# Two stage boundaries rewritten: norms by quarters, a fourth unit in the opening block, and quad operands prepared ahead of the norm

## The chip, the cores and the metric

The kernel runs on one core of one Trainium2 chip. The metric is device time in microseconds (us) for one execution. TensorE is called PE, VectorE DVE, ScalarE ACT, GpSimd POOL, and SyncE, which only issues transfers here, SP.

## The reference

One inference step of one layer over 640 tokens (512 of a prompt, 8 streams of 16), width 1024, all in fp32:

```
x <- LN1(alpha*x + 0.5*SwiGLU_1(x))
p = x @ W_in          # conv B, C, H | q | k | v | g | gate_conv | gate_ret
y_c = (B * causal_conv3(C*H)) @ W_conv_br
y_r = (groupnorm(retention(q, k, v)) * silu(g)) @ W_ret_br      # 4 heads, rotary q and k
h = (sigmoid(gate_conv)*y_c + sigmoid(gate_ret)*y_r) @ W_out
x <- LN2(alpha*x + h)
x <- LN3(alpha*x + 0.5*SwiGLU_2(x))
```

It also returns the last convolution inputs and the retention states.

## The kernel before

**Products.** Every fp32 operand is split in a high part (`xh`, `wh`: rounded copy, made by ACT or by a converting DMA) and a low part (`xl`, `wl`: the rest, made by DVE or POOL). A product is three matmuls, low*high, high*low, high*high (`mm3`, line 776; the matmul itself is line 771). The chip has one pass of some 110 numbered weight chunks of 128x1024: SP loads the raw chunk, POOL issues the DMA of its high part (`high`, L675), then makes its low part (`low`, L684). A chunk sits in one of three ring slots, or in an extra slot (3, 4: `raw_x`, `wh_x`, `wl_x`) that lies over the tiles `th`, `tl` when these are dead; `EXTRA_SLOT` says which chunks do, `slot_free` what a load waits for, `release_order` in which order the chunks come free.

**Stages.** FFN 1; the projections; four retention heads; the output product; FFN 2. The up products of both FFNs and the projections are mostly made as *quads* (a seven-product scheme over two halves of the tokens and of the rows). A quad needs four sums `n1, n2, t3, t4` of quarters of x (`x_sums`, tiles `t32`, `th`, `tl`), and six weight operands A11, S12, A12, S3, A22, S4: quarters of a loaded block `qraw`, and sums of them in `qs` (`quad_s`). POOL makes two of these sums (`sums`, L697 and L701), DVE two (`second_sum`, `fourth_sum`), ACT the high parts (`quad_hi_part`), DVE the low parts (`quad_lo_part`). The first products of a stage are plain *units* of one chunk (128 output rows, two halves of 320 tokens, 24 matmuls each).

**A boundary** (between FFN 1 and the projections, here boundary A, and between the output product and FFN 2, boundary B) ends one stage with a layer norm and starts the next:

- PE ends with the products `last_down` (A) or `out_products` (B). They serve tokens in two sets, *early* (tiles 0 to 2) and *late* (3 and 4), so that DVE can normalise the early ones while PE works on the late ones.
- DVE (`end_stage`): adds the residual (`down`, L1968), `bn_stats` (L2002), the inverse deviation, then two instructions a tile for scale and shift (L2014, L2017), which signal `z_ready`.
- PE transposes z tile by tile in two pieces of four 128x128 blocks (`to_T`, L1084; 6 early pieces, later 4 late ones). ACT copies each piece to `xh`, DVE makes `xl` from the piece and `xh` (signal `x_low`), ACT then copies the piece whole to `xin` (signal `x_kept`), which `x_sums` reads. A PSUM bank is free after that.
- PE runs `IDLE_UNITS` = 8 matmuls on a tile of ones after the early pieces, then the first three units (`first_units`) over the first half of the tokens; at `LATE_AT` (before the last k of unit 3) it transposes the late pieces; then it runs the second half of the three units, then a fourth unit in both halves, then quads (A) or the first down products (B, `first_down`, which wait for `h_ready`).
- POOL makes the low parts of the first chunks only after `z_ready` of the early tiles, that of the fourth after all tiles.
- The six operands of a stage's first quad are made after the norm; at B between the first units and the down products.

Each engine has its own instruction list and runs it in order. Nothing reorders work; counts of semaphores (`wait_ge`) join them.

Of the kernel before, what the change touches and what calls it, by code (L numbers as in the profile page):

```python
# [48 lines left out]
FIRST_IN_DEAD = (SECOND - DOWN_PARTS + 2, LAST - OUT_PARTS + 1, LAST - OUT_PARTS + 2)  # L49
# [194 lines left out]
EARLY_PIECES = [(t, q) for t in range(EARLY) for q in range(2)]  # L244
# [3 lines left out]
def transposed_bank(b, t, q):  # L248

    return b if t < EARLY else (b + 5 + LATE_PIECES.index((t, q))) % 8  # L250
# [13 lines left out]
def build_layer(nc, a):  # L264
# [3 lines left out]
    with ctx:  # L268
# [130 lines left out]
        for n, (raw_at, hi_at) in enumerate(((t_at[3], t_at[1]), (t_at[0], t_at[2]))):  # L399
# [21 lines left out]
        pool_sums, dve_sums = sem("pool_sums"), sem("dve_sums")  # L421
# [25 lines left out]
        x_kept, x_low = sem("x_kept"), sem("x_low")  # L447
# [86 lines left out]
        def _(sync):  # L534
# [26 lines left out]
            def ffn(k):  # L561
# [8 lines left out]
                if k == 1:  # L570
                    sync.wait_ge(merged_ready, KT)
                    for slot in range(4):
                        sync.wait_ge(state_out[slot], 32 * H)
                load_quad(2 * k)
                load_quad(2 * k)
                load(3)
                for g in range(1, len(GROUPS)):
                    into_dead = (k, g) == (0, len(GROUPS) - 1)
                    load(2)
                    load_quad(2 * k)  # L580
                    if not into_dead:
                        load(1)
                    for _ in range(3):
                        load_quad(2 * k)
                    load(2 if into_dead else 1)
# [69 lines left out]
            load(KT)  # L655
            ffn(1)
# [9 lines left out]
        def _(pool):  # L666
# [37 lines left out]

            def ffn(k):
                if k == 1:
# [5 lines left out]
                sums(2 * k)  # L712
                if k == 1:
# [8 lines left out]
                for g in range(1, len(GROUPS)):  # L722
                    into_dead = (k, g) == (0, len(GROUPS) - 1)
                    high(ck(2 if into_dead else 3))
                    for part in range(3):
# [3 lines left out]
                        if into_dead and part == 2:  # L729
                            high(ck(2))  # L730
                        low()
                    sums(2 * k)
                    low()

            def projections():
                sums(1)
# [6 lines left out]
                low()  # L743
                sums(1)
# [11 lines left out]
            low()  # L756
            ffn(1)
# [1728 lines left out]
```

## Time and profile before

| | |
|---|---|
| median of 3 runs | 1802.85 us (1801.83 to 1803.66) |
| profiled execution, its own time | 1801.98 us |
| its span in the trace | 1799.8 us |
| PE busy | 1777.6 us, 99% |
| DVE, ACT, POOL busy | 71%, 36%, 30% |
| DMA share at boundary B, before the output product ends | 16 engines all busy, 407 GB/s |

Slices of the profile show PE at 90% or more from start to end, so the time is PE's own work plus the places where it waits or runs products that serve nothing. Idle time of any other engine costs nothing by itself.

### The profile page before, as it was taken

The numbers are of one execution on the slowest core, as the hardware profiler recorded it, in microseconds if no ns is written. First come the engines' busy times: TensorE is split into PE (matmuls) and PEld (weight loads), VectorE is DVE, ScalarE is ACT, GpSimd is POOL, SyncE is SP. The second block draws the span as 40 slices with busy tenths as digits, with TensorE's granted clock in tenths as the row PEclk, the third lists the DMA queues.
The fourth block names the chain that finished last, engine by engine and source line by source line (L and its number), as shares of the span: only waits on it lengthen the run. The fifth ranks groups of instructions, "written<-read, shape, count | busy, mean of one in ns | idle before, by whom it ended". The sixth has DMA issues, their size and how long they took to land.

```text
span 1799.8 us, 26971 instructions
## 1 busy us (share of the span) xinstructions
PE 1777.6 (99%) x10868; PEld 1656.8 (92%) x10868; DVE 1281.2 (71%) x1698; ACT 645.0 (36%) x1102; POOL 541.1 (30%) x360
## 2 busy tenths in 40 slices
PE   9999999999999999999999999999999999999997
PEld 8989899898999999999998979798989989899896
DVE  7958485667798787776257666767867868485675
ACT  5425233242545454544106050514205325242242
POOL 2324242224232222121341323232244324233231
PEclk9999999999999999999999999999999999999998
DMA  7342423325443333422764958586964332323313
GB/s 272 129 141 71 141 73 132 123 71 199 146 143 127 115 130 101 143 87 91 273 240 140 339 200 312 204 284 231 345 258 158 129 135 77 129 82 129 114 63 106
DMA packets 89419, 287.33 MB, mean 160 GB/s; under 512 B 8784, under 2 KB 11216, under 8 KB 89040
## 3 DMA queue, kind: packets, MB, share of 16 engines
q1 hardware_dynamic: 48176, 171.72, 28.3%
q0 software_dynamic: 15552, 56.63, 9.2%
q10 hardware_dynamic: 25568, 57.26, 8.7%
q8 instruction: 87, 1.43, 0.3%
q14 instruction: 36, 0.29, 0.0%
HBM read 244.35 MB, written 42.28 MB: 159 GB/s over the span
## 4 chain that ended last, share of the span: by engine, by line
PE 91%; DMA 3%; POOL 1%; issue 1%; DVE 1%; ACT 1%; DVEq 0%; POOLq 0%
PE ps L771 90%; DMA wh<-in_weights 2%; PE ps L1141 1%; POOL wl L684 1%; DMA wh_x<-in_weights 1%; ACT xh L1282 0%; POOL wl_x L684 0%; DVE y L2075 0%; DVE z L2064 0%; PE ps L1084 0%; DVE y L2084 0%; ACT xin L1282 0%; DVE rt L1682 0%; DVE xl L1682 0%; DVE mv L2070 0%
## 5 line engine op out<-in xcount | busy, mean ns | idle before, releaser
L771 PE MATMUL ps<-th,wql 128*128 128x320 f32 x1136 | 350.9, 309 | 0.0
L771 PE MATMUL ps<-th,wqh 128*128 128x320 f32 x1136 | 350.7, 309 | 0.0
L771 PE MATMUL ps<-tl,wqh 128*128 128x320 f32 x1136 | 350.0, 308 | 0.0
L684 POOL TENSOR_TENSOR wl<-raw,wh 128x1024 fp32r<-128x1024 f32 x101 | 257.3, 2549 | 97.7 <-DMA wh<-in_weights 70.6
L1282 ACT ACTIVATE pu<-ps 128x320 f32<-128x320 f32 x213 | 93.3, 438 | 522.7 <-PE ps L771 522.6
L1682 DVE TENSOR_TENSOR wql<-qraw,wqh 128x512 fp32r<-128x512 f32 x213 | 259.9, 1220 | 17.3 <-ACT wqh L1282 17.1
L771 PE MATMUL ps<-xl,wqh 128*128 128x320 f32 x852 | 262.7, 308 | 0.0
L771 PE MATMUL ps<-xh,wqh 128*128 128x320 f32 x852 | 262.6, 308 | 0.0
L771 PE MATMUL ps<-xh,wql 128*128 128x320 f32 x852 | 262.5, 308 | 0.0
L697 POOL TENSOR_TENSOR quad_s<-qraw 128x512 f32<-128x512 f32 x71 | 93.7, 1319 | 485.2 <-DVE wql L1682 449.0
L1682 DVE TENSOR_TENSOR wql<-quad_s,wqh 128x512 fp32r<-128x512 f32 (+1 forms) x213 | 194.3, 912 | 45.3 <-ACT wqh L1282 44.5
L771 PEld LDWEIGHTS ps<-tl,wqh 128*128 128x128 f32 x1136 | 213.3, 188 | 0.4
L771 PEld LDWEIGHTS ps<-th,wql 128*128 128x128 f32 x1136 | 213.2, 188 | 0.4
L771 PEld LDWEIGHTS ps<-th,wqh 128*128 128x128 f32 x1136 | 213.2, 188 | 0.0
L675 POOL DMA_DIRECT2D wh<-in_weights x101 | 56.8, 563 | 515.2 <-PE ps L771 415.4
L1282 ACT ACTIVATE wqh<-quad_s 128x512 fp32r<-128x512 f32 (+1 forms) x213 | 163.8, 769 | 50.2 <-PE ps L771 50.2
L771 PE MATMUL ps<-wh,hl 128*128 128x512 f32 x430 | 168.2, 391 | 0.5 <-DVE sig L1682 0.2
L771 PE MATMUL ps<-wh,hh 128*128 128x512 f32 x430 | 167.6, 390 | 0.0
L771 PE MATMUL ps<-wl,hh 128*128 128x512 f32 x430 | 167.6, 390 | 0.0
L771 PEld LDWEIGHTS ps<-xl,wqh 128*128 128x128 f32 x852 | 160.0, 188 | 0.4
L771 PEld LDWEIGHTS ps<-xh,wql 128*128 128x128 f32 x852 | 159.9, 188 | 0.4
L771 PEld LDWEIGHTS ps<-xh,wqh 128*128 128x128 f32 x852 | 160.0, 188 | 0.0
(221 smaller groups left out, 3440.8 us busy)
## 6 DMA issues: line engine op xcount, KB each, us to landing
qraw<-in_quads SPq DMA_DIRECT2D x142, 512.0 KB, 3.6
raw<-in_weights SPq DMA_DIRECT2D x105, 512.0 KB, 3.8
wh<-in_weights POOLq DMA_DIRECT2D x101, 512.0 KB, 5.5
state<-in_state_ret ACTq DMA_DIRECT2D x32, 512.0 KB, 6.7
out_ret_sample<-state ACTq DMA_DIRECT2D x32, 512.0 KB, 5.2
state<-in_state_ret SPq DMA_DIRECT2D x16, 512.0 KB, 5.3
qk_scratch<-ctp SPq DMA_DIRECT2D x8, 640.0 KB, 5.4
swish_scratch<-ctp SPq DMA_DIRECT2D x6, 640.0 KB, 3.0
```

The source lines that it names most:

```text
L675: pool.dma_start(w_hi(r), a["weights"][c]).then_inc(hi_loaded[r], 16)
L684: pool.tensor_tensor(w_lo(r), w_raw(r), w_hi(r).bitcast(f32), ALU.subtract).then_inc(chunk_split, 1)
L697: pool.tensor_tensor(qs[:, 0, :], qraw[:, c0, 512:1024], qraw[:, c1, 512:1024], ALU.add).then_inc(pool_sums, 1)
L771: ins = nc.tensor.matmul(out, lhs, rhs, start=start, stop=stop, skip_group_check=adds)
L1141: last = nc.tensor.transpose(cols(k, 128, ps[:, b, :]), src, ident[:, :])
L1282: return nc.scalar.activation(out, in_, ACT.Copy, **kw)
L1682: return V.tensor_tensor(out, x, y, op)
```

## The change

It touches the two boundaries only; the arithmetic is the same.

- Four units instead of three (`FIRST_UNITS`) stand in the opening block, first halves first. The 8 idle products are gone.
- Unit 0 begins with the high*high products of quarter 0 (k 0 to 3), which need four high copies and one bank; then high*low, then quarter 1, and its chunk's low part last. Copies and low parts are ordered by quarters to match (`HIGH_ORDER`, `LOW_ORDER`, `natural_part`), and the transposed pieces lie in other banks (`EARLY_BANK`). Hence PE waits, ahead of the first transposition, until DVE has freed all but two banks.
- The fourth unit's products with the high part of its chunk stand before the late transpositions, the ones with its low part behind them.
- `second_sum` and `fourth_sum` of the first quad of the projections and of FFN 2 move from DVE to POOL (`all_sums`). At A it stands before the last `low` of FFN 1, at B behind the last `low` of the output product.
- Their six operands: ACT's high parts move ahead of the norm. DVE's low parts move too: at A two ahead of the norm, one behind the late shift, one behind the late `xl` pieces, two where they were; at B all six between the first and the second half of the early residual sums.
- The four loads of the first two quads of FFN 2 move on SP from behind three raw chunks of FFN 2 to right behind the last raw chunk of the output product; the loads of `z_kept` 3 and 4 move on ACT behind the first PSUM results of the output product.
- The last chunk of FFN 1 (25) instead of the third last (24) takes the extra slot; it is loaded after P7 of the last quad and not after P4. The extra slots' places over `tl` and the release order change with it. `x_sums` makes only n1 before the first chunk's release.

```diff
-FIRST_UNITS = 3
+FIRST_UNITS = 4
-IDLE_START, IDLE_UNITS = 24, 8
-LATE_AT = (FIRST_UNITS - 1, 7)
-DOWN_LATE, OUT_LATE = (2, 0, 1, 3), (1, 0, 3, 4, 2)
-EXTRA_SLOT = {SECOND - DOWN_PARTS + 2: NSPL, SECOND: NSPL,
+DOWN_LATE, OUT_LATE = (3, 0, 2, 1), (1, 0, 3, 4, 2)
+EXTRA_SLOT = {SECOND - 1: NSPL, SECOND: NSPL,
...
+T_HIGH_ORDER = (0, 2, 1, 3)
+T_LOW_ORDER = [(0, 1, 2, 3) if stage == 1 else (0, 2, 1, 3) for stage in range(3)]
+EARLY_PIECES = [(0, 0), (1, 0), (0, 1), (1, 1), (2, 0), (2, 1)]
+HIGH_ORDER = [(0, 0), (1, 0), (0, 1), (2, 0), (1, 1), (2, 1)]
+LOW_ORDER = [(t, q) for q in range(2) for t in range(EARLY)]
+EARLY_BANK = {(0, 0): 2, (1, 0): 4, (2, 0): 0, (0, 1): 1, (1, 1): 3, (2, 1): 5}
+HIGHS_BEFORE = {q: 1 + max(n for n, piece in enumerate(HIGH_ORDER) if piece[1] <= q) for q in range(2)}
...
-                engine.wait_ge(chain_full, chained(QUADS - 1, P4))
+                engine.wait_ge(chain_full, chained(QUADS - 1, P7))
...
             load(KT)
+            sync.wait_ge(merged_ready, KT)
+            for slot in range(4):
+                sync.wait_ge(state_out[slot], 32 * H)
+            load_quad(2)
+            load_quad(2)
             ffn(1)
...
+            def all_sums(stage):
+                n = qk.at
+                sums(stage)
+                pool.wait_ge(pool_sums, 2 * n + 1)
+                pool.tensor_tensor(qs[:, 1, :], qs[:, 0, :], quad_source(n, A11), ALU.add).then_inc(later_sums, 1)
+                pool.wait_ge(later_sums, 2 * n + 1)
+                pool.wait_ge(quad_ready, operand(n - 1, S4))
+                pool.tensor_tensor(qs[:, 3, :], qs[:, 1, :], quad_source(n, A12), ALU.add).then_inc(later_sums, 1)
...
                 high(ck(2))
                 low()
             low()
+            all_sums(2)
             ffn(1)
...
             def to_T(pieces):
-                kept = zr.at // TT * 2 * TT
+                if pieces is EARLY_PIECES:
+                    pe.wait_ge(psum_free, bk(EARLY - TT))
...
-                if pieces is EARLY_PIECES:
-                    pe.wait_ge(x_low, kept + 1)
-                    pe.wait_ge(x_kept, kept + 1)
-                    idle_products(IDLE_UNITS, bk(-2 * EARLY) % 8)
...
+                pe.wait_ge(hi_loaded[s0], 16 * loads_of_slot(ck.at, FIRST_HI))
+                pe.wait_ge(x_kept, kept + 1)
+                for q in range(2):
+                    ks = range(4 * q, 4 * q + 4)
+                    pe.wait_ge(x_high, kept + HIGHS_BEFORE[q])
+                    for k in ks:
+                        products(0, 0, k, (0, 0), k == 0, False)
+                    pe.wait_ge(x_low, kept + EARLY * (q + 1))
+                    for k in ks:
+                        products(0, 0, k, (0, 1), False, False)
+                assert chunk() == s0
+                for k in range(KT):
+                    products(0, 0, k, (1, 0), False, k == KT - 1)
...
+                for k in range(KT):
+                    products(u, 0, k, (0, 0), k == 0, False)
+                    products(u, 0, k, (0, 1), False, False)
+                late_tiles()
+                assert chunk() == s
+                for k in range(KT):
+                    products(u, 0, k, (1, 0), False, k == KT - 1)
+                for u in range(FIRST_UNITS):
+                    pe.wait_ge(x_kept, kept + 2 * EARLY + u + 1)
...
             act.wait_ge(sp_out, 16 * H)
+            act.wait_ge(psum_full, bk(EARLY))
+            for t in range(EARLY, TT):
+                kept_load(t)
+            for what in (A11, S12, A12, S3, A22, S4):
+                quad_hi_part(QUAD_START[2], what)
             bk.add(2 * TT)
             roots_and_to_T()
...
+                if k == 1:
+                    quad_lo_part(PROJ, A11)
+                    quad_lo_part(PROJ, S12)
                 for t in early:
                     if residual is z_kept:
                         dve.wait_ge(z_kept_in[t], 16)
                     down(scale, 0, [t], residual)
                     moments(0, [t])
+                if k == 2:
+                    for what in (A11, S12, A12, S3, A22, S4):
+                        quad_lo_part(QUAD_START[2], what)
                 for t in early:
                     down(scale, 1, [t], residual)
                     moments(1, [t])
...
                 inv_deviation(late)
                 scale_and_shift(late)
+                if k == 1:
+                    quad_lo_part(PROJ, A12)
                 to_T(LATE_PIECES)
+                if k == 1:
+                    quad_lo_part(PROJ, S3)
                 transposed_freed(k, late)
```

## Rows read from the trace of the kernel before

**Rows 1.** Timeline of PE at boundary A: start, us, engine, line, operation; idle before

```profile
416.75 0.50 PE L771 MATMUL ps<-wh_x,hl 128*128 128x512 f32 x1 [0.87 <-POOL wl_x L684]
...
435.93 2.78 PE L1084 MATMUL ps<-ident,z 128*128 128x128 f32 x24
440.24 1.41 PE L771 MATMUL ps<-ones 128*128 128x320 f32 x8 [1.53 <-ACT xin L1282]
441.49 0.31 PE L771 MATMUL ps<-xh,wl_x 128*128 128x320 f32 x1
...
455.02 0.41 PE L771 MATMUL ps<-xh,wl_x 128*128 128x320 f32 x1 [0.84 <-ACT xin L1282]
...
472.72 0.31 PE L771 MATMUL ps<-xh,wql 128*128 128x320 f32 x1
```

**Rows 2.** Timeline of ACT at boundary A

```profile
436.56 3.05 ACT L1282 ACTIVATE xh<-ps 128x512 fp32r<-128x512 f32 x6 [9.07 <-PE ps L1084]
439.44 3.11 ACT L1282 ACTIVATE xin<-ps 128x512 f32<-128x512 f32 x6
...
452.24 2.24 ACT L1282 ACTIVATE xh<-ps 128x512 fp32r<-128x512 f32 x4 [6.29 <-PE ps L1084]
```

**Rows 3.** Timeline of DVE at boundary A

```profile
418.44 0.69 DVE L1968 SCALAR_TENSOR_TENSOR z<-ps,z 128x512 f32<-128x512 f32 x1 [3.98 <-PE ps L771]
...
437.42 3.67 DVE L1682 TENSOR_TENSOR xl<-ps,xh 128x512 fp32r<-128x512 f32 x6
```

**Rows 4.** Timeline of POOL at boundary A

```profile
452.17 2.38 POOL L684 TENSOR_TENSOR wl<-raw,wh 128x1024 fp32r<-128x1024 f32 x1 [7.49 <-DVE z L2017]
```

**Rows 5.** Timeline of PE at boundary B

```profile
1353.95 2.78 PE L1084 MATMUL ps<-ident,z 128*128 128x128 f32 x24
...
1372.88 0.42 PE L771 MATMUL ps<-xh,wl_x 128*128 128x320 f32 x1 [0.90 <-DVE xl L1682]
...
1390.58 0.39 PE L771 MATMUL ps<-wh,hl 128*128 128x512 f32 x1
```

**Rows 6.** Timeline of POOL at boundary B

```profile
1331.92 2.40 POOL L684 TENSOR_TENSOR wl<-raw,wh 128x1024 fp32r<-128x1024 f32 x1 [0.19 <-DMA wh<-in_weights]
...
1359.97 1.29 POOL L697 TENSOR_TENSOR quad_s<-qraw 128x512 f32<-128x512 f32 x1
...
1384.16 0.53 POOL L675 DMA_DIRECT2D wh<-in_weights  x1 [2.95 <-PE ps L771]
1385.70 2.42 POOL L684 TENSOR_TENSOR wl<-raw,wh 128x1024 fp32r<-128x1024 f32 x1 [1.02 <-DMA wh<-in_weights]
```

**Rows 7.** Timeline of ACT at boundary B, operand S12 of FFN 2's first quad

```profile
1384.12 1.05 ACT L1282 ACTIVATE wqh<-quad_s 128x1024 fp32r<-128x1024 f32 x1
```

**Rows 8.** Timeline of DVE at boundary B and behind it

```profile
1337.82 0.69 DVE L1968 SCALAR_TENSOR_TENSOR z<-ps,z_kept 128x512 f32<-128x512 f32 x1 [12.84 <-PE ps L771]
...
1351.57 1.28 DVE L2017 SCALAR_TENSOR_TENSOR z<-z,rt,lnb 128x1024 f32<-128x1024 f32 x1
...
1386.47 2.34 DVE L1682 TENSOR_TENSOR hl<-h,hh 128x640 fp32r<-128x640 f32 x1 [0.81 <-ACT hh L1282]
...
1392.79 0.82 DVE L1682 TENSOR_TENSOR hl<-h,hh 128x640 fp32r<-128x640 f32 x1 [0.81 <-ACT hh L1282]
...
1399.66 1.22 DVE L1682 TENSOR_TENSOR wql<-quad_s,wqh 128x1024 fp32r<-128x1024 f32 x1
```

**Rows 9.** Busy time by stretch: PE, PEld, DVE, ACT, POOL, clock, DMA, GB/s

```profile
1322.00:1328.00 6.00, 5.57 (x26) 4.29 (x24) 2.92 (x5) 0.00 (x0) 2.61 (x3) 1.00 1.06 407
...
1788.00:1790.00 2.00, 0.26 (x2) 0.00 (x0) 1.93 (x7) 0.48 (x3) 0.61 (x1) 1.00 0.94 96
1790.00:1792.00 2.00, 0.00 (x0) 0.00 (x0) 2.00 (x2) 1.16 (x2) 0.00 (x0) 0.66 1.07 201
```

**Rows 10.** Timeline of SP at the end of the output product

```profile
1312.84 7.13 SPq L542 DMA_DIRECT2D raw<-in_weights  x2
```

**Rows 11.** Timeline of PE at the start of the kernel

```profile
1.26 5.67 PE L771 MATMUL ps<-ones 128*128 128x320 f32 x24 [1.26 <-DVE ones L2130]
```

More of the change, by code:

```diff
@@ L569, in ffn @@
                 load(2)
[L570 to L575, printed above, removed]
+                if k == 0:
+                    load_quad(0)
+                    load_quad(0)
                 load(3)
                 for g in range(1, len(GROUPS)):
-                    into_dead = (k, g) == (0, len(GROUPS) - 1)
                     load(2)
                     load_quad(2 * k)
-                    if not into_dead:
-                        load(1)
+                    load(1)
                     for _ in range(3):
                         load_quad(2 * k)
-                    load(2 if into_dead else 1)
+                    load(1)
             def spill(q):
@@ L728, in ffn @@
                             pool.wait_ge(c22_made, QUAD_START[2 * k] + QUADS - 1)
-                        if into_dead and part == 2:
-                            high(ck(2))
                         low()
-                    sums(2 * k)
+                    if (k, g) == (0, len(GROUPS) - 1):
+                        all_sums(1)
+                    else:
+                        sums(2 * k)
                     low()
             def projections():
-                sums(1)
                 high(ck(4))
@@ L1054, in ffn @@
                     idle_products(IDLE_START, 0)
-                for u in range(0 if first else FIRST_UNITS, 4):
-                    unit_of_chunk(x_wait=x_piece if first and u == 0 else None)
+                for u in range(FIRST_UNITS if first else 0):
+                    unit_of_chunk(x_wait=x_piece if u == 0 else None)
                 n = 0 if first else QUAD_START[2]
@@ L1103, in first_units, with products @@
                 own, kept = bk.at, (zr.at - EARLY) * 2
-                slots = []
-                w_ofs = [lambda k, u=u: (cols(k, 128, w_hi(slots[u])), cols(k, 128, w_lo(slots[u])))
-                         for u in range(FIRST_UNITS)]
-                def before_half(half):
-                    pass
+                used = []
+                def products(u, half, k, which, start, stop):
+                    s, c = used[u], slice(half * HALF, (half + 1) * HALF)
+                    w_part, x_part = which
+                    w_of, x_of = (w_hi(s), w_lo(s))[w_part], (xh, xl)[x_part]
+                    return mm(ps[:, (own + 2 * u + half) % 8, 0:HALF], cols(k, 128, w_of), x_of[:, k, c], start, stop)
                 def late_tiles():
@@ L1126, in before_unit @@
+                for u in range(1, FIRST_UNITS - 1):
+                    used.append(chunk())
+                    if u == 1:
+                        pe.wait_ge(x_kept, kept + 2)
                     else:
                         pe.wait_ge(psum_free, own - 10)
[L1129 to L1134 removed]
@@ L1331, in window @@
                 bk.add(2)
-                quad_hi_part(n, A11)
-                quad_hi_part(n, S12)
+                if ffn == 0:
+                    quad_hi_part(n, A11)
+                    quad_hi_part(n, S12)
                 plain_hi(2 * ffn)
-                for what in (A12, S3, A22, S4):
-                    quad_hi_part(n, what)
+                if ffn == 0:
+                    for what in (A12, S3, A22, S4):
+                        quad_hi_part(n, what)
                 act.wait_ge(psum_free, bk())
@@ L1902, in projections @@
                 banks_freed(4)
-                for what in (A11, S12, A12, S3, A22, S4):
-                    quad_lo_part(n, what)
+                quad_lo_part(n, A22)
+                quad_lo_part(n, S4)
                 second_sum(n + 1)
@@ L2028, in end_stage @@
                     moments(0, [t])
+                if k == 2:
+                    for what in (A11, S12, A12, S3, A22, S4):
+                        quad_lo_part(QUAD_START[2], what)
                 for t in early:
@@ L2123, in to_T, with highs @@
                        xh[:, part[0], part[1]].bitcast(f32), ALU.subtract).then_inc(x_low, 1)
+                bk.add(len(pieces))
+            def highs(low, piece):
+                return low if piece in LATE_PIECES else (low - 1) // (2 * TT) * 2 * TT + HIGH_ORDER.index(piece) + 1
             def first_low_part(c, made, part=slice(0, D)):
```

173 lines of the change are left out of this document (98 added, 75 removed).

## The prediction

> **What bounds the kernel now.** I read the page first: PE is busy 99% of the span, so only what PE waits for, or runs for nothing, can be won. The timeline of PE then shows where that is. At boundary A [rows 1] PE waits 0.87 us for chunk 24's low part (DVE's sums follow PE there: DVE had been idle 3.98 us when it began, rows 3). It then transposes 24 blocks (2.78 us), waits 1.53 us, runs 8 products of ones that serve nothing, and starts real products at 441.49, 5.56 us after the first transposition. Behind the late transpositions it waits once more, until 455.02. Boundary B [rows 5] has the same shape: transpositions from 1353.95, the second halves only at 1372.88, the first down product at 1390.58. In sum some 5 us at A and 4.5 us at B can be won, 0.5% of the time. The rest of the trace matters only where the change makes another engine late. For that I read the timelines of ACT, DVE, POOL and SP around both boundaries [rows 2 to 4, 6 to 8, 10]. A product of 320 columns costs 0.147 us: from 455.02 to 472.72 there are 120 of them [rows 1].
>
> **Boundary A.** Times here count from the first transposition, T = 435.93 in the trace.
>
> *Chunk 24.* It no longer lies in the extra slot, so its data are there long before. Chunk 25 does, but its load starts one product group earlier (P7, not P4: 12 products of 0.147 and six of the lead, some 3 us) and PE needs it 4 us later than chunk 24. POOL's sums for the first quad of the projections stand in a stretch in which POOL waits. Won: 1.0 us (the start-to-start gap is 1.25 us where 0.23 is usual). DVE's two early low parts, 0.6 and 1.2 us, fit in its 3.98 us of idle time [rows 3]; without that cover they would cost 1.8 us.
>
> *Start of unit 0.* ACT's first copy starts at +0.63 and each takes 0.51 [rows 2], the pieces arrive every 0.44. The fourth high copy is that of the fifth piece: 2.4 to 3.0. The natural copy of the first piece follows, 2.9 to 3.5, and PE starts at +3.7 instead of +5.56. DVE's low parts go from +1.49 at 0.61 each [rows 3]: the third is done at 3.7, in time; the sixth waits for ACT's last high copy (4.5) and is done at 5.6, where PE is at 5.4. Unit 0 ends at 7.4 instead of 9.1.
>
> *Units 1 to 3.* Two units of 3.53, then 16 products: +16.8 (it was +15.8). The late tiles are shifted at +16.2, where POOL starts the fourth low part [rows 4], so the 16 transpositions run without a wait and end at +18.6. But DVE's low part of A12 now stands right there, too, and reads two SBUF operands as POOL does. Rows 8 show what that means: `hl` next to POOL's `low` [rows 6] took 2.34 us, alone 0.82. I let POOL lose the 0.7 us: its part is ready at 19.35, 8 products end at 20.6. The first natural copy of a late piece lets PE go 2.78 after ACT's first late copy [rows 1, 2], here at +20.2, earlier. So the second halves start at 20.6 with 96 products left: 34.7. Before: 455.02 is +19.1, with 120 left: +36.8. Won: 2.1 us. The next in line is DVE: it must wait for chunk 26's release (24.1), make three x sums and four low parts (4.2 and 5.7 us) before it frees the units' banks, at about +34.3; 0.4 us of slack are left, which I cost at nothing.
>
> A gives 3.1 us, between 1.5 (POOL and bank late by 0.8 each) and 4.
>
> **Boundary B.** This is where I expect the change to pay back. `all_sums` stands behind the last `low` of the output product, which ends at 1334.3 [rows 6]. All six low parts of the first quad's operands stand on DVE between the early tiles' first and second halves, and DVE starts the second half at 1337.82, having waited 12.84 us for PE [rows 8]. The chain that must now fit between the two: POOL's sums at 1.28 each [rows 6], the third of which S12 needs (3.9 us), ACT's high part of S12 (1.05, rows 7), DVE's low part of it (1.22, rows 8), and four more at 0.61 with the gaps of signals: 8.7 us in all. From 1334.3 that ends at 1343.0. And POOL's last `low` will be later: until 1328 the 16 DMA engines are fully busy at 407 GB/s [rows 9], and behind the last raw chunk (about 1319.6 to 1320, rows 10) SP now issues four loads of 512 KB, 5.2 us of all engines; the last high part's DMA shares with them. I put it at 1.1 us (nothing to 2.2). So DVE begins its second half at 1344.1, 6.3 us late.
>
> What follows, by the distances of the old trace: the residual of the late tiles' first half is done at 1350.2 + 6.3 = 1356.5 (L2017 of tile 2, rows 8, ends at 1352.85, and the shift's two instructions take 2.6 of it). PE waits for it now ahead of its transpositions, for which it is ready at 1353.95 or some 0.5 earlier: 3 us of idle time. Tile 2 is shifted at 1359.1, two `bn_stats` follow (1.3), the first `xl` 0.65, the natural copy 0.6: unit 0 starts at 1361.9. From there PE needs 96 products, 1.85 us of transpositions and two short waits (0.5 at the sixth `xl`, 0.5 at the late natural copy): the second halves start at 1378.8, and end at 1392.9, where before they ended at 1390.58.
>
> Then the down products start, and all before them has less cover than it had: three units of second halves were followed by 48 products, now by one unit. The high parts of the down chunks need the slots of units 1 and 2: before, the second was issued at 1384.16 and the low part made from 1385.70 [rows 6], 11.3 and 12.8 us after the second halves' start; that is 1391.6 to 1394.0 now. On DVE and ACT `x_sums` wait for unit 0 (1382.6), then three sums, the last high part, a table load, sigmoid and the plain tile give `h_ready` at 1394.0, plus 0.75 for `hl` next to POOL's `low`, as in rows 8. The second down chunk's low part costs 0.4 more. The down products so start at 1394.8, effectively 1395.3: B loses 4.7 us, between 2.5 (no DMA delay, no collision) and 6.
>
> The Trainium skill states this collision as a rule (page "SBUF — State Buffer", section "SBUF: two separate sides"): GpSimd and a DVE instruction with two SBUF inputs take one port in turn, whole instructions long. The trace agrees, 2.34 against 0.82 us. By a kernel without it, the sum would be 1.1 us less.
>
> **The sum** is made against the profiled execution: 1801.98 - 3.1 + 4.7 = 1803.6. That execution was 0.87 below the median of the runs, so I forecast 1804.4, 0.1% above the median. A measurement of this kernel can tell some 0.2%, 3.6 us, from no change. The bounds give 1801.5 to 1806.9 as the likeliest case's own range.
>
> **The rivals.**
>
> *The norm at B is not delayed.* POOL would have to finish its sums before 1333 or so, or DVE the operands in its idle time. The same sums move at A, and there they fit. Against it: at B the sums stand behind a `low` that ends at 1334.3 in the trace. Then B is as A: unit 0 starts 1.9 us sooner and the idle products are gone, 2.4 us, and 0.6 for the wait of a chunk in the output product. Sum: -3.1 - 3.0 = 1796.7. Chance 0.12.
>
> *The clock falls at B.* At the end of the trace PE's last product ends at 1788.26, and the granted clock is 1.00 until 1790 and 0.66 on average to 1792 [rows 9]: it went from 2.4 to 1.2 GHz some 2.4 us behind the last product. The gaps of 1.53 us it held through. By my sum PE is idle for 3 us ahead of the transpositions and twice more up to unit 0. At half rate the first 24 products of the kernel took 5.67 us instead of 3.53 [rows 11], 2.1 us more; the tail of the transpositions adds up to 0.9. That gives 1804.4 + 3.0 = 1807.4, slower. It decides from the point where PE's gap exceeds about 2.4 us. Against it: transpositions run in between, and the fall may end before unit 0 starts, and then costs under 1 us. Chance 0.22. The Trainium skill, page "TensorE: Matmul & The Clock Gate", section "Why this matters for your kernels", warns of just this: idle gaps between bursts of products bring the half clock back. No row before has a gap as long within the kernel.
>
> *A gives only chunk 24's 1.0 us.* POOL and DVE collide longer, or the banks come late. Then 1806.5. Chance 0.1.
>
> The forecast itself: 0.56.
>
> **Numbers.** Faster by over 0.2% (below 1799.2) is the first rival and little else: 0.13. Slower (above 1806.5): two thirds of the clock's case, half of the third rival, a tenth of the forecast: 0.27. The same: 0.60. The range leaves out the first rival and the clock's worst: 1800 to 1808.
>
> **What the profile will show.** Right: no wait for `wl_x` near 415; PE's first `xh` product 3.7 us behind the first transposition at A and the first quad 34.7; at B DVE's first residual with `z_kept` of the second half near 1344 behind `wql` low parts, an idle PE of some 3 us ahead of the transpositions, and a wait of the first down product for POOL's or DVE's part. Wrong: DVE's second half at B still started by PE at about 1337; or `quad_s` on POOL done before 1335; or PE waiting at A for a bank ahead of the first quad, or for chunk 25.

## The result and the profile after

| | before | changed |
|---|---|---|
| median, both timed in turn on one chip, 20 runs each | 1803.34 us (1801.38 to 1805.25) | 1806.20 us (1804.67 to 1808.69) |
| ratio, with its 95% interval | | 1.0018 (1.0011 to 1.0024) |
| profiled execution, its span | 1801.98, 1799.8 us | 1808.0, 1806.2 us |

The change costs 0.18%, inside what I called "the same" (0.2%), and lies in the forecast range. The changed kernel's profiled execution is 1.8 us above its own median, the one before 1.4 below its own, so the traces show a larger difference, 6.0 us, than the medians, 2.9. Small numbers from one trace are therefore checked against a second trace of the same kernel (`t_again` below).

**Boundary A** went as planned but for one wait. The timeline of PE in the changed kernel, to be read beside [rows 1]:

```profile
416.02 0.47 PE L796 MATMUL ps<-wh,hl 128*128 128x512 f32 x1 [0.39 <-DVE hl L1754]
...
435.19 2.78 PE L1116 MATMUL ps<-ident,z 128*128 128x128 f32 x24
438.75 0.83 PE L796 MATMUL ps<-xh,wh_x 128*128 128x320 f32 x4 [0.78 <-ACT xin L1338]
...
454.25 1.43 PE L796 MATMUL ps<-xh,wl 128*128 128x320 f32 x8 [0.29 <-POOL wl L698]
...
469.71 0.39 PE L796 MATMUL ps<-xh,wql 128*128 128x320 f32 x1
```

Counted from the first transposition, unit 0 starts at +3.56 (5.56 before), the last 8 products ahead of the second halves at +19.06, the first quad at +34.52. The first quad comes at 469.71 and not at 472.72: 3.0 us. But chunk 24 still waits, now for `hl`, and the reason stands in the timelines of DVE and of POOL:

```profile
409.76 3.16 DVE L1754 TENSOR_TENSOR ct<-ct,ct 128x1280 f32<-128x1280 f32 x1
```
```profile
409.17 2.39 POOL L698 TENSOR_TENSOR wl_x<-raw_x,wh_x 128x1024 fp32r<-128x1024 f32 x1 [4.38 <-DMA wh_x<-in_weights]
```

DVE's product of two SBUF tiles took 3.16 us; the same one took 1.49 in the kernel before, where POOL made no low part at that time:

```profile
410.01 1.49 DVE L1682 TENSOR_TENSOR ct<-ct,ct 128x1280 f32<-128x1280 f32 x1
```

The early low part of chunk 25 made it late, and `hl` behind it.

**Boundary B** went as feared, and further. The timelines of PE [rows 5], POOL [rows 6], ACT [rows 7] and DVE [rows 8], now:

```profile
1325.56 0.50 PE L796 MATMUL ps<-wh_x,xl 128*128 128x512 f32 x1 [1.43 <-POOL wl_x L698]
...
1355.85 1.97 PE L1116 MATMUL ps<-ident,z 128*128 128x128 f32 x16 [2.80 <-DVE z L2041]
1358.58 1.06 PE L1116 MATMUL ps<-ident,z 128*128 128x128 f32 x8 [0.77 <-DVE z L2090]
1360.95 1.35 PE L796 MATMUL ps<-xh,wh_x 128*128 128x320 f32 x4 [1.31 <-ACT xin L1338]
...
1394.68 0.50 PE L796 MATMUL ps<-wh,hl 128*128 128x512 f32 x1 [1.62 <-DVE hl L1754]
```
```profile
1325.46 0.58 POOL L689 DMA_DIRECT2D wh<-in_weights  x1
...
1332.62 2.39 POOL L698 TENSOR_TENSOR wl<-raw,wh 128x1024 fp32r<-128x1024 f32 x1 [2.19 <-DMA wh<-in_weights]
1334.97 1.29 POOL L711 TENSOR_TENSOR quad_s<-qraw 128x512 f32<-128x512 f32 x1
1336.22 1.30 POOL L715 TENSOR_TENSOR quad_s<-qraw 128x512 f32<-128x512 f32 x1
1337.47 1.29 POOL L724 TENSOR_TENSOR quad_s<-quad_s,qraw 128x512 f32<-128x512 f32 x1
```
```profile
1338.86 1.06 ACT L1338 ACTIVATE wqh<-quad_s 128x1024 fp32r<-128x1024 f32 x1 [12.18 <-POOL quad_s L724]
```
```profile
1339.95 1.27 DVE L1754 TENSOR_TENSOR wql<-quad_s,wqh 128x1024 fp32r<-128x1024 f32 x1 [12.54 <-ACT wqh L1338]
...
1342.95 0.68 DVE L1754 TENSOR_TENSOR wql<-quad_s,wqh 128x512 fp32r<-128x512 f32 x1
1343.55 0.68 DVE L2041 SCALAR_TENSOR_TENSOR z<-ps,z_kept 128x512 f32<-128x512 f32 x1
```

Read from the bottom up: DVE's second half of the norm (1343.55) stands behind its low parts. The one of S12 (1339.95) waited 12.54 us for ACT, which waited for POOL's third sum, which stands behind the last `low`, which waited for a transfer issued 7.2 us earlier. In the kernel before that transfer's low part started 4.05 us after the issue (1331.92 in [rows 6]):

```profile
1327.87 0.57 POOL L675 DMA_DIRECT2D wh<-in_weights  x1
```

PE, in turn, waits 2.80, 0.77 and 1.31 us.

Then something the medians alone wouldn't show, by stretch (PE, PEld, DVE, ACT, POOL, clock, DMA, GB/s):

```profile
1322.00:1328.00 6.00, 4.57 (x21) 3.44 (x20) 0.69 (x1) 0.63 (x1) 2.88 (x2) 1.00 1.05 412
1328.00:1334.00 6.00, 5.47 (x24) 4.20 (x23) 0.00 (x0) 0.00 (x0) 3.75 (x2) 1.00 0.49 188
...
1360.00:1362.00 2.00, 1.05 (x4) 1.08 (x5) 2.00 (x5) 1.75 (x4) 2.00 (x2) 0.75 0.00 0
1362.00:1364.00 2.00, 2.00 (x10) 2.00 (x9) 2.00 (x5) 2.00 (x5) 2.00 (x2) 0.50 0.00 0
```

The granted clock falls to 1.2 GHz right at the start of unit 0, for 3.41 us by the clock's record, and unit 0's 24 products take 5.13 us where 24 such products take 3.53 at full clock.

### The profile page after: what moved, and what is told of

It reads as the page before. It is cut to its first block and busy times, and to the rows that moved or that the text cites. A ratio compares the mean times of both kernels' runs of the same rounds, so it can differ in the third digit from the quotient of the medians.

```text
span 1806.2 us, 26935 instructions
## 1 busy us (share of the span) xinstructions
PE 1779.4 (99%) x10852; PEld 1655.6 (92%) x10852; DVE 1284.0 (71%) x1694; ACT 645.7 (36%) x1102; POOL 550.1 (30%) x364
```

## The experiments

My theory **N**: at B the norm is late, because it stands behind the operands' chain. Rivals: **C**, the clock's fall is what costs; **D**, the transfers are, by way of the output product's own low weights. The first four kernels take boundary B back step by step.

The table holds all fourteen traces of twelve kernels (`t_again` and `b4_again` repeat one each). All times are starts on PE in the one trace of each: "to B" is the start of the extra slot's chunk in the output product (its first `wh_x` high*high product), "B" the time from there to the first down product of FFN 2, "rest" from there to PE's last product. Ratios are to the kernel before, timed in turn on the same chip; every interval reaches 0.0006 to 0.0011 to either side. A trace is one execution, so differences of some tenths between traces show nothing by themselves.

| trace | ratio | to B | B | rest |
|---|---|---|---|---|
| before | 1 | 1323.75 | 66.83 | 397.30 |
| changed | 1.0018 | 1320.34 | 74.34 | 398.28 |
| t_again | 1.0015 | 1319.85 | 72.96 | 397.91 |
| b1_dve | 0.9988 | 1320.89 | 67.76 | 397.84 |
| b2_act | 0.9984 | 1319.01 | 67.64 | 397.93 |
| b3_pool | 0.9988 | 1320.14 | 68.09 | 398.68 |
| b4_sp | 0.9975 | 1319.91 | 65.46 | 398.00 |
| b4_again | 0.9980 | 1320.11 | 66.20 | 397.99 |
| c1_warm | 1.0015 | 1320.05 | 72.91 | 397.85 |
| c2_warm | 1.0011 | 1320.32 | 72.31 | 397.83 |
| d_kept | 1.0023 | 1321.44 | 72.04 | 397.87 |
| a_ops | 0.9993 | 1323.99 | 66.51 | 398.01 |
| all3 | 0.9981 | 1320.63 | 66.05 | 397.64 |
| a_two | 0.9982 | 1320.04 | 66.13 | 398.00 |

### b1_dve: DVE's six low parts at B made late again

```diff
-                if k == 2:
-                    for what in (A11, S12, A12, S3, A22, S4):
-                        quad_lo_part(QUAD_START[2], what)
...
-                if k == 0:
-                    quad_lo_part(n, A11)
-                    quad_lo_part(n, S12)
+                quad_lo_part(n, A11)
+                quad_lo_part(n, S12)
```

(and so for the other four, among the down residuals)

> The changed kernel with one step of its boundary B undone: DVE makes its six low quadrant parts later, among the down residuals, instead of ahead of the second half of the norm. ACT's high parts, POOL's sums and SP's quadrant loads stay early. Theory N (the norm's second half is late because it stands behind DVE's six parts, which stand behind ACT's six, which stand behind POOL's sums): DVE's second half starts some 3 us late instead of some 9, because ACT's root still stands behind its six parts; TensorE's idle time at the early transposes falls from 2.8 us to under 1; some 2 to 3 us come off, 1803.2 to 1804.2 against 1806.2. Theory C (the cost is TensorE's clock record, at half rate for 3.4 us): nothing but the 1.6 us of slow products comes off, and only if the clock stays whole. Theory D (the cost is that the quadrant loads share the DMA rings with the out product's weights): no change within 0.5 us, for those loads stay where they are.

Measured 1800.33 us (1797.8 to 1803.82) against 1802.72, ratio 0.9988 (0.9979 to 0.9997): some 5 us less than the changed kernel's ratios put it. One edit on DVE turns the loss into a small gain. D falls as the main cause, since the loads did not move. C could claim 1.6 at best. N holds, but its price was more than the 2 to 3 us that I expected, because ACT's parts did not hold the root up by 3 us:

```profile
1336.87 0.69 DVE L2038 SCALAR_TENSOR_TENSOR z<-ps,z_kept 128x512 f32<-128x512 f32 x1 [14.74 <-PE ps L796]
...
1342.24 0.18 DVE L2059 RECIPROCAL rt<-rt 128x3 f32<-128x3 f32 x1 [0.64 <-ACT rt L1478]
```
```profile
1341.50 0.62 ACT L1338 ACTIVATE wqh<-quad_s 128x512 fp32r<-128x512 f32 x1
1342.02 0.19 ACT L1478 ACTIVATE rt<-rt 128x3 f32<-128x3 f32 x1
```

DVE's residuals and `bn_stats` of the second half (1336.87 to 1341.43) run beside ACT's six parts; the root comes 0.4 us late, and PE's wait ahead of the transpositions is gone. With it the clock stayed whole at B.

### b2_act and b3_pool: ACT's high parts, then POOL's sums, late again too

```diff
 # b2_act
-            for what in (A11, S12, A12, S3, A22, S4):
-                quad_hi_part(QUAD_START[2], what)
             bk.add(2 * TT)
 # b3_pool, also
             low()
-            all_sums(2)
             ffn(1)
```

(Not shown: b3_pool puts `sums(2)` back on POOL behind three low parts of FFN 2, and gives `second_sum` and `fourth_sum` back to DVE.)

> As b1_dve, with ACT's six high parts back in the stretch ahead of the first MLP products too; POOL's sums and SP's loads stay early. Theory N: the norm is on time again, no clock drop, and what is left of B's cost is the out product's own extra waits for low weights, some 2 us (1.43, 0.53 and 0.17 us of waits against 0.6 in all before): 1802.0 to 1803.0. Theory D: still no change from the changed kernel, 1806. Theory C: 1804.6 at best.

> As b2_act, with POOL's four sums back behind three low parts and two of the quadrant sums back with DVE, so that at B only SP's two quadrant loads and the two late residual loads are early. Theory N: the sums alone cost nothing once no one of ACT and DVE waits for them ahead of the norm, so within 0.4 us of b2_act; a rival is that POOL's early sums delay the first low part of the MLP, then 0.5 to 1 us come off here.

Measured 1799.84 us, 0.9984 (0.9975 to 0.9993), and 1800.24 us, 0.9988 (0.9979 to 0.9997). b2_act came out 2 us below the least that I expected of it (1802.0); b3_pool is within the 0.4 us of b2_act that I expected. Neither differs from b1_dve beyond the intervals. So ACT's parts and POOL's sums in themselves cost nothing at their new places that could be seen here; what stood behind them on DVE did.

### b4_sp: SP's quadrant loads late again

```diff
             load(KT)
-            sync.wait_ge(merged_ready, KT)
-            for slot in range(4):
-                sync.wait_ge(state_out[slot], 32 * H)
-            load_quad(2)
-            load_quad(2)
             ffn(1)
```

(they stand behind FFN 2's first three raw chunks again)

> As b3_pool, with SP's quadrant loads back behind the first plain loads of the second MLP: what is left is the change at boundary A, and the one at B only in its residual loads. If the quadrant loads hold up the low parts of the out product (last high-weight transfer 7.0 us from issue to landing against 3.9 before), TensorE's waits there go from some 2.6 us back to 0.6 and the time falls by 1.5 to 2 us against b3_pool, to 1800.0 to 1801.0; this prices boundary A by itself at a gain of 2.5 to 3. If the rival holds, that boundary A gives only 1.0, it ends at 1802.3. If the extra waits come from the residual loads instead, it stays with b3_pool.

Measured 1797.93 us (1796.84 to 1800.41), 0.9975 (0.9965 to 0.9986); as `b4_again` 1799.1 us, 0.9980 (0.9971 to 0.9989). That is 1 to 3 us better than I expected. Against b3_pool it is 1.4 to 2.3 us; the intervals of the ratios still overlap, so the traces must support it. The timeline of POOL in b4_sp, and in b3_pool:

```profile
1323.58 0.57 POOL L687 DMA_DIRECT2D wh<-in_weights  x1
...
1328.29 2.39 POOL L696 TENSOR_TENSOR wl<-raw,wh 128x1024 fp32r<-128x1024 f32 x1 [1.71 <-DMA wh<-in_weights]
```
```profile
1324.61 0.57 POOL L689 DMA_DIRECT2D wh<-in_weights  x1
...
1332.21 2.38 POOL L698 TENSOR_TENSOR wl<-raw,wh 128x1024 fp32r<-128x1024 f32 x1 [2.72 <-DMA wh<-in_weights]
```

From issue to low part it is 4.7 us without the quadrant loads and 7.6 with them. In b3_pool PE waits three times in the output product (0.78, 0.44 and 0.73 us), in b4_sp not at all. What is left of the change in b4_sp, boundary A and, at B, the new order of the units and the late residual loads, gains 3.6 to 4.5 us. No run takes the quadrant loads back alone, with the low parts still ahead of the norm (these need the loads), so how much of the changed kernel's loss the loads make through that chain is read from its traces and not from a run.

### t_again and c1_warm: the clock

`t_again` is the changed kernel unaltered.

> The changed kernel itself once more, as the frame for c1_warm, and to see in a second trace whether the drop of the granted clock at boundary B is regular. Both theories: 1.0018 of the time before, within its interval. Theory N (a late norm is the cause, the clock comes with it): TensorE waits again some 2.8 us ahead of the early transpositions, and the granted clock falls to 0.5 again for some 3.4 us at unit 0. If the record shows no drop here and the median is the same, the clock has no part in the median.

Measured 1805.29 us, 1.0015 (1.0006 to 1.0023). PE waits 2.79 us ahead of the transpositions, and the clock falls again, from 1359.26 for 3.41 us, at unit 0. The wait stands in both traces. For the clock there is more: each timed execution has a mean granted clock, rounded to a thousandth. It is 0.9974 to 0.9976 on average in the sets of the kernel before, 0.9969 over the 20 executions of the changed kernel and 0.9967 over the 11 of t_again. A fall of 3.41 us to half takes some 0.0009 off such a mean (an estimate, 3.41 / 2 over 1804 us), so the fall is regular.

```diff
 # c1_warm
                 if pieces is EARLY_PIECES:
+                    if zr.at:
+                        pe.wait_ge(psum_free, bk(EARLY - 2 * TT))
+                        idle_products(18, bk.at % 8)
                     pe.wait_ge(psum_free, bk(EARLY - TT))
```

> The changed kernel with 18 products of ones on TensorE at boundary B, in the stretch in which it waits for the norm ahead of the early transpositions (2.6 us of work in 3.2 us of waiting). The real work and every wait stay. Theory C (the drop of the clock costs time of its own): the clock stays at 1.0, the 24 products of unit 0 take 3.5 us and not 5.1, and 1.6 us come off, to 1.0009 of the time before. Rival: the granted clock falls anyway, for the two gaps of 0.9 and 1.5 us around the last transpositions are still there; or the second halves wait for the late tiles' copies anyway; then the same time as t_again within 0.5 us.

Measured 1805.96 us, 1.0015 (1.0006 to 1.0024). The rival held: the time is t_again's, and in this trace the clock fell all the same. By stretch, the same columns as above:

```profile
1358.00:1360.00 2.00, 0.69 (x5) 0.56 (x4) 2.00 (x5) 1.59 (x4) 2.00 (x2) 0.97 0.00 0
1360.00:1362.00 2.00, 2.00 (x9) 2.00 (x9) 2.00 (x4) 2.00 (x5) 2.00 (x2) 0.50 0.00 0
1362.00:1364.00 2.00, 2.00 (x11) 2.00 (x10) 1.97 (x4) 0.80 (x2) 2.00 (x1) 0.68 0.04 8
```

In this execution the long stall was filled, so the 2.8 us of idle time are not needed to bring the clock down. But the trace is not a typical one. Its execution has a mean clock of 0.996, the lowest of the 11 of c1_warm; four others have 0.998, which no execution of the changed kernel has and one of t_again's 11. Their average is 0.9973, beside 0.9974 in the same set's kernel before. In a good part of the executions, then, the filled stall seems to have held the clock, and the time was the same all the same.

### c2_warm: one more stall filled

```diff
+                kept_b = zr.at
...
                 for t, q in pieces:
+                    if pieces is EARLY_PIECES and kept_b and (t, q) == (2, 0):
+                        idle_products(6, (bk.at - 4) % 8)
                     b = bank()
```

> c1_warm with 6 more products of ones, on TensorE between the transpositions of the second and the third early tile (a stall of 0.9 us). At boundary B only the last stall of 1.5 us, ahead of unit 0, stays empty, as long as the one that the kernel before had there [rows 5] and came through at full clock. Theory C (the drop comes from the sum of TensorE's idle time around the transpositions, and costs time): the granted clock stays at 1.0, the 24 products of unit 0 take 3.5 us, and the time falls by 1.6 us against c1_warm, to 1.0006 of the time before. If the clock falls here too, it takes more than the stalls to hold it up, and the price of the drop stays what the slow products show. If it stays up and the time is that of c1_warm, the drop is free.

Measured 1804.37 us (1803.82 to 1807.0), 1.0011 (1.0003 to 1.0020), where 1.0006 was expected. In the trace the clock stayed at 1.0 up to the kernel's end. PE's timeline:

```profile
1352.24 2.80 PE L796 MATMUL ps<-ones 128*128 128x320 f32 x18
1355.14 1.97 PE L1122 MATMUL ps<-ident,z 128*128 128x128 f32 x16
1356.86 1.12 PE L796 MATMUL ps<-ones 128*128 128x320 f32 x6
1357.87 1.06 PE L1122 MATMUL ps<-ident,z 128*128 128x128 f32 x8
1360.24 0.82 PE L796 MATMUL ps<-xh,wh_x 128*128 128x320 f32 x4 [1.31 <-ACT xin L1344]
...
1362.55 0.86 PE L796 MATMUL ps<-xl,wh_x 128*128 128x320 f32 x4 [0.32 <-DVE xl L1760]
```

Unit 0's 24 products now take 4.18 us, not 3.53: at full clock PE runs into the wait for DVE's last `xl`, which half clock had covered. The fall costs 5.12 - 4.18 = 0.94 us and not 1.6. From the inverse deviation of the early tiles to the first down product it is 45.31 us here and 46.41 in c1_warm, 1.1 less. The ratios point the same way but their intervals overlap, and the mean clock of all 11 executions is 0.9975 here and 0.9973 in c1_warm. So these two runs show what a fall costs, in one trace each; they do not show that it was the six products that held the clock.

### d_kept: the two late residual loads early again

```diff
-            for t in range(EARLY):
-                kept_load(t)
-                merge_hi([4 + t])
-            merge_hi([KT - 1])
+            for t in range(TT):
+                kept_load(t)
+                if t < KT - 4:
+                    merge_hi([4 + t])
...
-            act.wait_ge(psum_full, bk(EARLY))
-            for t in range(EARLY, TT):
-                kept_load(t)
```

> The changed kernel with the two late loads of the residual (512 KB each) back where the kernel before issues them, some 8 us earlier, so that only the four quadrant loads share the DMA engines with the last high weights of the output product. Theory D+N (each us by which these weights land late makes POOL's last low part, its four sums, DVE's six low parts and the norm's second half late by one): 1 MB at some 410 GB/s is 2.5 us; the last low part and DVE's second half come up to 2.5 us earlier, TensorE's stall ahead of the transpositions falls from 2.9 to some 0.5 us, the clock holds, and 2.5 to 4 us come off: 1.0002 to 0.9996 of the time before. Rival: the residual loads, issued last, do not hold up the weights, or the early loads crowd another transfer: within 0.7 us of the changed kernel, 1.0013 to 1.0020.

Measured 1806.89 us (1804.97 to 1807.84), 1.0023 (1.0013 to 1.0033). My dose test failed: nothing came off, as the rival said (its range ended at 1.0020). The last high part was issued at 1325.75 and its low part began at 1332.77, 7.0 us, where the changed kernel has 7.2 and t_again 7.8. Issued earlier, the residual loads pushed others back: the raw chunks took 8.0 us to land and not 6.3 (medians of four), and ACT's first quadrant part came at 1328.9 and not at 1326.0. So it seems that all that is queued up to them sets what the last low weights lose, and not the loads issued last. The trace gives one more thing about the clock. Here it fell 2 to 4 us earlier, at 1357.26, within the transpositions:

```profile
1355.96 2.49 PE L1116 MATMUL ps<-ident,z 128*128 128x128 f32 x16 [2.75 <-DVE z L2038]
1358.69 1.94 PE L1116 MATMUL ps<-ident,z 128*128 128x128 f32 x8 [0.25 <-DVE z L2087]
1361.06 0.82 PE L796 MATMUL ps<-xh,wh_x 128*128 128x320 f32 x4 [0.43 <-ACT xin L1338]
```

PE's waits shrank from 0.77 and 1.31 to 0.25 and 0.43, and unit 0 began 5.10 us behind the first transposition, as in the changed kernel. From the inverse deviation of the early tiles to the first down product it is 45.34 us, as in c2_warm, where the clock stayed whole (45.31). A fall that met waiting cost nothing here.

### a_ops: the operands at A late again

```diff
 # on b4_sp; likewise ACT's six high parts behind x_hi_parts(1), POOL's all_sums(1) -> sums(1)
                 x_sums(1)
+                second_sum(n)
+                fourth_sum(n)
                 x_lo_parts(1)
                 dve.wait_ge(gate_made, 2)
                 banks_freed(4)
-                quad_lo_part(n, A22)
-                quad_lo_part(n, S4)
+                for what in (A11, S12, A12, S3, A22, S4):
+                    quad_lo_part(n, what)
```

> b4_sp with the operands of the projections' first quad made late again (POOL's sums and ACT's parts behind the norm, the two other sums with DVE behind its x sums, all six low parts behind the freed banks): boundary A keeps the four units, the quarters and the late low part alone. Theory O (at A the early operands are what lets the quads follow the fourth unit without a wait): DVE's two sums, 1.4 us, stand ahead of the low parts of x and the freed banks, where TensorE had 0.1 us of slack, and six low parts, 4.6 us, stand behind it with the first product needing the second of them: TensorE waits 1.5 to 4 us ahead of and within the first quad, 1799.5 to 1802.0 against 1797.9. Rival: the quads' first products hide them, within 0.5 us of b4_sp.

Measured 1801.71 us (1800.11 to 1803.42), 0.9993 (0.9984 to 1.0002), 2.3 to 3.2 us above b4_sp's ratios. Theory O holds, with a second part that I had not seen. In "to B" all that the change gains is gone again (1323.99 against 1323.75). PE waits 1.65 us at the first quad:

```profile
472.32 0.42 PE L792 MATMUL ps<-xh,wql 128*128 128x320 f32 x1 [1.65 <-DVE wql L1750]
```

and chunk 24 comes at 417.04, 1.0 us later than in the changed kernel, because POOL's sums now follow its low part of chunk 25, and both meet DVE's last work on h:

```profile
409.70 3.44 DVE L1750 TENSOR_TENSOR ct<-ct,ct 128x1280 f32<-128x1280 f32 x1
414.61 2.28 DVE L1750 TENSOR_TENSOR hl<-ct,hh 128x1280 fp32r<-128x1280 f32 x1 [1.47 <-ACT hh L1334]
```

### all3 and a_two: a better version?

```diff
 # all3, on b4_sp (at B also: the sigmoid ahead of three of ACT's x parts)
+                    if (k, g) == (0, len(GROUPS) - 1):
+                        pool.wait_ge(h_ready, 2 + 2 * PAIRS)
                     low()
...
                 banks_freed(4)
+                quad_lo_part(n, A12)
+                quad_lo_part(n, S3)
                 quad_lo_part(n, A22)
```

> b4_sp with three small waits taken out: POOL makes chunk 25's low part only behind DVE's last split of h (so that it does not slow DVE's sum and chunk 24's products wait no more, 0.35 us there), the low parts of A12 and S3 at A stand behind the freed banks (POOL's low part is not slowed, 0.4 us), and at B ACT takes the sigmoid of the first down tile before three of the four high parts of x, DVE its two quadrant sums behind that tile (TensorE's wait of 1.4 us for the first down tile, of which the low part of that chunk, ready at 1384.6, leaves 0.7 to be won). Each wait is real time if nothing else ends right behind it: 1.2 to 2 us off, 1796.0 to 1796.8 in b4_sp's frame, 0.9966 of the time before. Rival: each wait hides another by the next engine; within 0.5 us of b4_sp.

Measured 1799.76 us, 0.9981 (0.9973 to 0.9990). The expectation fell. `low` itself issues the transfer of its chunk's high part, so my wait held that up, too: it was issued at 414.54 instead of some 404, and PE waited 1.14 us for chunk 25. At B the split of h ended at 1383.0 and not at 1385.3, in a trace that is 1.4 us later there, so 3.7 us sooner; but the chunk's own low part was the next limit (POOL, 1383.67 to 1386.58), and PE's start-to-start gap was 1.44 us, where b4_sp had 1.56.

```diff
 # a_two: the same without the edit at B, and with
+                        high(ck.at + 1)
                         pool.wait_ge(h_ready, 2 + 2 * PAIRS)
```

> b4_sp once more, as the frame for a_two and because its gain of 4.8 us is more than the 2.5 to 3 that I expected of boundary A. If the gain is real: 0.9975 of the time before again, between 0.997 and 0.998. If the earlier set of runs was lucky by its chip: 0.9983.

> b4_sp with two waits at boundary A taken out: POOL issues the transfer of chunk 25's high part as before, but makes its low part only behind DVE's last split of h, so that DVE's sum of 1.5 us does not take 3.0; and the low parts of A12 and S3 stand behind the freed banks. (In all3 the first of these held the transfer up too, and TensorE waited 1.3 us for it.) Theory: 0.35 and 0.45 us of TensorE's waits are real time, 0.8 us off b4_again, 0.9970 of the time before. Rival: POOL's late low part now meets DVE's split of h or the low parts of A11 and S12, and nothing is won: within 0.4 us of b4_again.

Measured 1799.1 us for b4_again (ratio above) and 1799.08 us for a_two, 0.9982 (0.9973 to 0.9991): the same. The rival held. (For b4_again 0.9975 was to confirm the first measurement and 0.9983 to call it lucky; 0.9980 lies between, at the edge of what I had allowed.) DVE's product took 1.49 us again and chunk 24's wait was gone, but POOL's low part met the low part of S12 instead, and the norm came later:

```profile
414.66 3.43 DVE L1751 TENSOR_TENSOR wql<-quad_s,wqh 128x1024 fp32r<-128x1024 f32 x1
```
```profile
434.45 1.91 PE L1117 MATMUL ps<-ident,z 128*128 128x128 f32 x16
436.98 1.06 PE L1117 MATMUL ps<-ident,z 128*128 128x128 f32 x8 [0.62 <-DVE z L2086]
```

So b4_sp stays the version to keep, 3.6 to 4.5 us under the kernel before; all3 and a_two are as fast and no faster.

## Why the prediction was right

The time and the verdict came out as forecast, and so did the mechanism at both boundaries. The sum, though, had B's loss too small, by more than the range that I gave that term, and A's gain slightly too large.

- **A, the units.** Unit 0's start (+3.7 forecast, +3.56 measured), its end (+7.4, +7.48) and the first quad (+34.7, +34.52) are right. DVE freed the banks at 469.49, just in time, as the 0.4 us of slack said. a_ops shows that this gain rests on the early operands.
- **A, chunk 24.** Forecast 1.0 us; its start-to-start gap fell from 1.25 to 0.77, so 0.5. I had priced the collision of POOL and DVE at the late shift, but not the one that the early low part of chunk 25 itself makes, 3.16 against 1.49 us. POOL's fourth low part took 2.76 us [rows 4: 2.38], so 0.4 and not 0.7 was lost there. An instruction of DVE and one of POOL that both read two SBUF tiles slow each other here. The Trainium skill's rule (page "SBUF — State Buffer", section "SBUF: two separate sides") says that they share a port; the trace agrees (3.16 against 1.49 us), and a_two shows that moving one party only picks another victim.
- **A in sum.** Forecast 3.1. "To B" says 3.4 and 3.9 in the two traces of the changed kernel, of which 0.3 to 0.4 stem from the first product's start, and 0.6 from a shorter wait at 1035 that has nothing to do with the change. What is left is 2.5 and 2.9 us, slightly less than forecast, as chunk 24's half would have it.
- **B, the transfers: the mis-sized term.** I put the delay of the last low part at 1.1 us (0 to 2.2). Counted from the extra slot's chunk, it starts at 8.17 us before and at 12.28 and 11.24 now: 4.1 and 3.1 late. b3_pool and b4_sp show the cause: 7.6 us from issue to low part with the quadrant loads, 4.7 without. I had counted bytes sharing the engines with one transfer; in fact the weights that PE needed earlier were late as well, with waits of 1.43 and 0.53 us in the output product (one of 1.29 in t_again). b4_sp prices the quadrant loads at 1.4 to 2.3 us where the norm does not stand behind them.
- **B, the norm.** Forecast 6.3 us late, measured 9.1 and 8.1: the chain from the last `low` took what I gave it, and the excess is the transfers' term. PE's wait ahead of the transpositions was forecast at 3 us and measured at 2.80. b1_dve removes the chain with one edit and gets some 5 us back.
- **B, the down products.** The wait for `hl` next to POOL's `low` came (1.62 us, `hl` at 1.44 and not at the 2.34 of rows 8).
- **B in sum.** Forecast 4.7 (2.5 to 6); measured 7.5 and 6.1, beyond my bound. The rest of the kernel adds 1.0 and 0.6 that I cannot place; every trace but the one before shows 0.3 to 1.4 there, b4_sp's too.
- **The clock.** The rival's event happened, in every trace of the changed kernel, and the forecast's mechanism with it; I had made them exclusive. But I priced it at 3.0, and c2_warm shows 0.9, d_kept nothing. My point of decision, a gap of over 2.4 us, was wrong: in c1_warm's trace no idle time around the transpositions was over 1.30 us. Nor were rows 11 a price of the half clock: the record shows 1.00 there, and the same 24 products took 5.08 to 6.56 us among the fourteen traces; 24 products under the fall itself took 5.12. The Trainium skill's warning against idle gaps (page "TensorE: Matmul & The Clock Gate", section "Why this matters for your kernels") agrees in its direction: in the changed kernel the fall came behind stalls of 2.80, 0.77 and 1.31 us.
- **The sum** of 1803.6 says 1.6 us more than before. The two traces of the changed kernel have spans 6.4 and 2.5 us longer (1806.2 and 1802.3 against 1799.8), the medians 2.9 and 2.2. B's excess of 2.8 and 1.4 us should have shown in them, for A gave none of it back. The fair pair of traces is the one before and t_again's, 1.4 and 1.2 us below their medians. There PE's last product comes 2.8 us later: 6.1 at B and 0.6 behind it, less 2.9 at A, less 1.0 from the first product and the wait at 1035, which is in no term of the sum. So the sum came near the medians partly by luck. The two bounds of the forecast don't follow from its own terms either: with A between 1.5 and 4 and B between 2.5 and 6 they are 1801.3 and 1807.4, not 1801.5 and 1806.9.

What stays open: why d_kept's ratio is the highest, when its B is not; its trace has a wait of 1.8 us at 1037 that varies from 0 to 1.8 among all the traces. And what, beside the long stall, decides whether the clock falls at B: there is one trace each of the kernels that fill stalls.

## What to carry to other kernels

Work made early is free only up to the first instruction that it stands in front of: price the whole chain that feeds it (transfer, POOL, ACT, DVE), not its own duration, and put it behind the norm's critical part when its input may be late. Transfers issued early into a stretch where all DMA engines are full delay the ones that are needed next (7.6 us against 4.7 from issue to low part here). When a change touches two places, take back one place, step by step: here what b4_sp keeps gained some 4 us, and what it takes back had lost 6 to 8.

## What the runs showed of the hardware that I had not expected

- The granted clock fell to 0.5 in all four traces in which PE had two or three stalls around B's early transpositions (the changed kernel twice, c1_warm, d_kept), each time for 3.41 us. In c1_warm's trace PE was idle only 0.77 and 1.30 us there; in c2_warm's, with the first of these filled, the clock held. By the mean clocks of all executions the fall is regular in the changed kernel and in d_kept (0.9967 to 0.9969), and not in c1_warm (0.9973). The kernel before had 1.53 us of idle time behind 24 unbroken transpositions, and held it.
- A fall of the clock cost what was left after the waits that it covered: 0.94 us at unit 0, where the products themselves took 1.6 us more, and nothing within the transpositions.
- Next to POOL's two-operand work, DVE's two-operand instructions of 1.49 us took 2.3 to 3.7 (3.16 for the product at A), one of 1.22 took 3.43, and POOL's own, mostly 2.4, took up to 3.3 (413.43 in the kernel before, 3.27 us).
